# First two units behind each of three norms computed together in two PSUM banks, and the third unit's remainder made before the norm

## What is computed

```
x = x + g1 * rms_norm(y, norm_g[i, 1])                       # y = merged branches @ w_o
h = rms_norm(x, norm_g[i, 2]) * (1 + sc2) + sh2              # norm 1 of the change
x = x + g2 * rms_norm(square(relu(h @ mlp_up)) @ mlp_down, norm_g[i, 3])
...
h = rmsnorm(x, g_mix[l]) * (1.0 + sc1) + sh1                 # norm 2: second block's mixer
x = x + gt1 * hybrid_mixer_2(h, w_in[l], ...)
h = rmsnorm(x, g_ffn[l]) * (1.0 + sc2) + sh2                 # norm 3: second block's FFN
x = x + gt2 * conv_glu_ffn(h, w_ffn_gate[l], w_ffn_up[l], ...)
```

## Time and profile before

| | before |
|---|---|
| median of 3 runs | 3558.66 us (3558.66 to 3563.43) |
| profiled execution | 3559.49 us, its span 3557.8 us |
| mean granted TensorE clock | 0.981 |
| busy: TensorE / VectorE / ScalarE | 3349.8 / 2133.4 / 1159.6 us |
| MLP: first unit starts, third unit starts | 1647.98, 1666.38 |
| MLP: starts of quarters 2, 3, 4 | 1844.99, 2030.67, 2214.61 |
| In2: first unit starts, third unit starts | 2426.27, 2446.86 |
| Ffn2: first unit starts, third unit starts | 2788.17, 2806.15 |
| memsets L2414 and L3052 on VectorE, each | 3.47 us |

### The profile page before, as it was taken

The page is one execution under the profiler, slowest core; times in us unless marked ns, Lnnn a source line. Parts: engine busy times, 40 slices in busy tenths (PEclk is TensorE's granted clock), DMA queues, the critical chain, the costliest instruction groups (busy, mean ns, idle before and its releaser), DMA issues. The chain is left out here.

```text
span 3557.8 us, 57477 instructions
## 1 busy us (share of the span) xinstructions
PE 3349.8 (94%) x23146; PEld 2742.8 (77%) x23146; DVE 2133.4 (60%) x3166; ACT 1159.6 (33%) x1462; POOL 166.9 (5%) x277
## 2 busy tenths in 40 slices
PE   6898989989998999988999999998999899999998
PEld 3673676467777899976888888886888788888887
DVE  2184654653333566556877777777655766666565
ACT  2111031022222322144434343434443444344343
POOL 0000000111221000000000000000000000000000
PEclk9999999999999999999999999999999999999999
DMA  9754624712212587734777777773444455555554
GB/s 370 312 213 164 260 99 172 289 66 82 70 41 82 185 316 308 289 133 155 263 277 272 272 273 279 275 273 103 158 154 155 140 189 189 189 186 185 186 179 138
DMA packets 99122, 706.25 MB, mean 199 GB/s; under 512 B 10992, under 2 KB 10992, under 8 KB 17776
## 3 DMA queue, kind: packets, MB, share of 16 engines
q1 hardware_dynamic: 74736, 523.27, 41.3%
q0 software_dynamic: 23184, 169.88, 13.0%
q10 hardware_dynamic: 1008, 10.23, 0.7%
HBM read 697.05 MB, written 6.29 MB: 198 GB/s over the span
## 5 line engine op out<-in xcount | busy, mean ns | idle before, releaser
L2282 PE MATMUL ps<-hT_parts,rows_parts 128*128 128x512 f32 x3300 | 1170.3, 396 | 0.0
L2281 PE MATMUL ps<-hT_parts,ring_parts 128*128 128x256 f32 x3300 | 934.4, 283 | 3.2 <-DVE hT_parts L2225 3.2
L2247 DVE TENSOR_TENSOR ring_parts<-ring,rows_parts 128x2048 fp32r<-128x2048 f32 (+1 forms) x340 | 769.8, 2265 | 222.4 <-ACT rows_parts L2242 221.5
L2242 ACT ACTIVATE rows_parts<-ring 128x2048 fp32r<-128x2048 f32 (+1 forms) x340 | 643.3, 1894 | 463.6 <-DMA ring<-in_mlp_u 218.3
L2282 PEld LDWEIGHTS ps<-hT_parts,rows_parts 128*128 128x128 f32 x3300 | 624.8, 189 | 128.4
L2281 PEld LDWEIGHTS ps<-hT_parts,ring_parts 128*128 128x128 f32 x3300 | 628.6, 190 | 25.2 <-DVE hT_parts L2225 14.8
L2282 PE MATMUL ps<-work_parts,rows_parts 128*128 128x512 f32 x1616 | 574.5, 397 | 0.0
L2281 PE MATMUL ps<-work_parts,ring_parts 128*128 128x256 f32 x1616 | 453.7, 281 | 0.0
L535 PE MATMUL ps<-hT,ring 128*128 128x512 f32 (+1 forms) x1088 | 377.0, 508 | 16.9 <-ACT work L802 12.6
L2282 PEld LDWEIGHTS ps<-work_parts,rows_parts 128*128 128x128 f32 x1616 | 304.3, 188 | 68.3
L535 PEld LDWEIGHTS ps<-hT,ring 128*128 128x128 f32 x1088 | 207.0, 191 | 185.3 <-issue 173.7
(11 more groups left out here) (432 smaller groups left out, 3627.4 us busy)
## 6 DMA issues: line engine op xcount, KB each, us to landing
ring<-in_mlp_u SPq DMA_DIRECT2D x128, 1024.0 KB, 5.2
ring<-in_ffn_u SPq DMA_DIRECT2D x88, 1024.0 KB, 4.9
rows<-in_mod_r POOLq DMA_DIRECT2D x64, 1024.0 KB, 6.1
ring<-in_gate_u SPq DMA_DIRECT2D x64, 1024.0 KB, 6.6
work<-in_ada_r POOLq DMA_DIRECT2D x64, 1024.0 KB, 5.4
ring<-in_in_u SPq DMA_DIRECT2D x36, 1024.0 KB, 4.9
ring<-in_mod_u SPq DMA_DIRECT2D x32, 1024.0 KB, 7.8
rows<-in_ada_r POOLq DMA_DIRECT2D x32, 1024.0 KB, 7.7
```

Of the source, the lines that this page charges most:

```text
L2242: act.activation(unit_high(u)[:, 0:size], slot(u)[:, 0:size], ACT.Copy).then_inc(hi_done, 1)
L2247: dve.tensor_tensor(ring_parts[:, u % SLOTS, 0:size], slot(u)[:, 0:size], unit_high(u)[:, 0:size].bitcast(F32), ALU.subtract)\
L2281: pe.matmul(ps[:, b, low_half], low, top(kt), start=False, stop=False)
L2282: mm = pe.matmul(ps[:, b, :], high, both(kt), start=False, stop=kt == kts - 1)
```

## The change

`twin_products` does two units K-tile by K-tile, each in its own bank. It waits at its head for both remainders and both banks. It stands for the first two units at three places: in the MLP loop as `n == 0` (thus in each of the four quarters), at the head of In2, and at the head of Ffn2, whose next two units are written out and whose loop begins at 1. The remainder of the third unit is made by VectorE before the norm's reciprocal; inside the MLP loop that of the next quarter's third unit stands at the end of the body.

```
+        def twin_products(pe, u, uses, x, off=0, it=None, k=0, split=0):
+            both, top, low_half = x
+            for o in range(2):
+                pe.wait_ge(w_split, off + (u + o - SPLIT0 + 1))
+                acquire(pe, uses[o], it, k)
+            for kt in range(KT):
+                pe.wait_ge(x_split, split + kt + 1)
+                columns = slice(kt * P, (kt + 1) * P)
+                for o in range(2):
+                    b = uses[o][0]
+                    high, low = w_high[:, (u + o) % SLOTS, columns], ring_parts[:, (u + o) % SLOTS, columns]
...
+                        pe.matmul(ps[:, b, low_half], low, top(kt), start=False, stop=False)
+                        mm = pe.matmul(ps[:, b, :], high, both(kt), start=False, stop=kt == KT - 1)
+                    if kt == KT - 1:
+                        mm.then_inc(w_used, 1)
# Mix.vector
                 add_scaled(dve, own, yT1, gn1)
+                rest_unit(dve, seg_mlp + AHEAD_DVE)
                 rms_x1.vector(dve)
# Mlp.tensor, in the loop over q and n
-                        unit_products(pe, seg_mlp + n, (n % 2, use_mlp[n % 2][1] + n // 2), x, q * (2 * KT), q, KT,
-                                      split=KT if n == 0 else None, ready=hidden_ready)
+                        if n == 0:
+                            twin_products(pe, seg_mlp, use_mlp, x, q * (2 * KT), q, KT, split=KT)
+                        elif n > 1:
+                            unit_products(pe, seg_mlp + n, (n % 2, use_mlp[n % 2][1] + n // 2), x, q * (2 * KT), q, KT, ready=hidden_ready)
# Mlp.vector
-                        if n != KT - 1:
+                        if n not in (0, KT - 1):
                             rest_unit(dve, seg_mlp + n + AHEAD_DVE, q * (2 * KT))
...
+                    rest_unit(dve, seg_mlp + 2 * KT + AHEAD_DVE, q * (2 * KT))
# In2.tensor
-                for n in range(36):
-                    unit_products(pe, seg_in2 + n, in2_use(n), low_then_high(hT_parts), split=2 * KT if n == 0 else None)
+                twin_products(pe, seg_in2, [in2_use(n) for n in range(2)], low_then_high(hT_parts), split=2 * KT)
+                for n in range(1, 36):
+                    if n > 1:
+                        unit_products(pe, seg_in2 + n, in2_use(n), low_then_high(hT_parts))
# Ffn2.tensor
+                    if n == 0:
+                        twin_products(pe, seg_ffn[0], use_ffn[0], low_then_high(hT_parts), split=4 * KT)
+                        for j in range(2, 4):
+                            unit_products(pe, seg_ffn[0] + j, (j % 2, use_ffn[0][j % 2][1] + 1), low_then_high(hT_parts))
-                    with pe.Fori(0, tiles // 2) as it:
+                    with pe.Fori(0 if n else 1, tiles // 2) as it:
# Ffn2.vector
+                rest_unit(dve, seg_ffn[0] + AHEAD_DVE)
                 rms_x3.vector(dve)
```

More of the change, by code:

```diff
@@ L2283, in unit_products @@
             mm.then_inc(w_used, 1)
+        def twin_products(pe, u, uses, x, off=0, it=None, k=0, split=0):
[9 more added lines that the diff above has]
+                    high, low = w_high[:, (u + o) % SLOTS, columns], ring_parts[:, (u + o) % SLOTS, columns]
+                    if kt == 0:
+                        pe.matmul(ps[:, b, :], high, both(kt), start=True, stop=False)
+                        pe.matmul(ps[:, b, low_half], low, top(kt), start=False, stop=False)
+                    else:
+                        pe.matmul(ps[:, b, low_half], low, top(kt), start=False, stop=False)
+                        mm = pe.matmul(ps[:, b, :], high, both(kt), start=False, stop=kt == KT - 1)
+                    if kt == KT - 1:
+                        mm.then_inc(w_used, 1)
         FIRST, SECOND = slice(0, T), slice(T, 2 * T)
@@ L2880, in vector @@
                     t = IN2_ORDER[n]
-                    rest_unit(dve, seg_in2 + n + AHEAD_DVE)
+                    if n:
+                        rest_unit(dve, seg_in2 + n + AHEAD_DVE)
                     large_add(dve, n + 1, n % 2, u2[:, t:t + 1, :], SECOND, in2_half)
@@ L2979, in tensor @@
                 for n, tiles in enumerate(PARTS2):
-                    with pe.Fori(0, tiles // 2) as it:
+                    if n == 0:
[3 more added lines that the diff above has]
+                    with pe.Fori(0 if n else 1, tiles // 2) as it:
                         for j in range(4):
-                            unit_products(pe, seg_ffn[n] + j, (j % 2, use_ffn[n][j % 2][1] + j // 2), low_then_high(hT_parts), it * 4, it, 2,
-                                          split=4 * KT if n + j == 0 else None)
+                            unit_products(pe, seg_ffn[n] + j, (j % 2, use_ffn[n][j % 2][1] + j // 2), low_then_high(hT_parts), it * 4, it, 2)
                     done += tiles
@@ L3074, in hidden @@
                             u = seg_ffn[n] + 2 * r
-                            rest_unit(dve, u + AHEAD_DVE, it * 4, size_of(u + AHEAD_DVE + (2 * tiles - 4 if end else 0)))
+                            if n or r or not begin:
+                                rest_unit(dve, u + AHEAD_DVE, it * 4, size_of(u + AHEAD_DVE + (2 * tiles - 4 if end else 0)))
                             large_add(dve, at + 1, 0, gpad[:, r:r + 1, FFN_TAPS - 1:], SECOND, gate_half)
```

## The result

The changed kernel takes 3574.2 us in the median of 8 runs (3573.13 to 3585.53), the kernel before 3559.41 in the median of 8 (3556.97 to 3570.89). The ratio is 1.0042, 95% interval 1.0030 to 1.0054. The profiled execution took 3573.51 us with a span of 3571.8, where that of before had 3557.8: +14.0 us.

A forecast was written before the change was run, and what follows sets the result against it. VectorE's chain was taken to bound the MLP's up half. Terms +2.2 + 15.7 - 3.4 - 2.2 gave +12.3 on 3559.49 us, 3571.8; with the median 0.8 lower, the forecast was 3571.0 us, range 3565 to 3577.

The forecast's parts named there:

- What bounds the kernel: MLP up half: VectorE's rigid chain needs 11.88 us per pair of units, TensorE 11.2, so VectorE's start sets the quarter's end.
- The three later quarters: MLP loop, quarters two to four: the twin delays the first unit's end and VectorE's chain by 5.24 us each, +15.7 us.
- The first quarter: MLP norm and first quarter: no gain; late row lands later, behind weight transfers, +2.2 us (0 to +4.5).
- a term near +1: First quarter: alternative size if DMA engines alternate between queues and the late row passes the second weight unit.
- In2: Second block's input norm: twin ends both units at 2440.0 instead of 2443.28, -3.4 us.
- FFN: FFN norm: third unit starts 2.2 us sooner, its first bank free only after VectorE's memset, -2.2 us.
- The remainder ahead of the norm: Before the norms' reciprocals: the 2.29 us remainder hides in VectorE's idle time, 2.39 us at the MLP; 0, at most +0.3.
- A sign of being wrong that did come: Changed kernel's trace: a granted clock falling inside the up halves was named as one sign against the forecast.
- A: Whole kernel faster: TensorE's own waits count and VectorE's late start is soaked up; -5.1 us, 3553.6; chance 0.07.
- B: Nearly no change: ScalarE's 1.38 us wait leaves VectorE's chain, so TensorE recovers 4.2 us a quarter; 3558 us; chance 0.07.
- C: Slower, less so: later quarters cost in full, late row on time, In2's clock at once; +8.2 us, 3566.9; chance 0.13.
- D: Worse: late row lands behind both transfers, and transfer pairs collide in each quarter; up to +21, typically 3577 us; chance 0.10.

The follow-up runs named there:

- The stall experiment: Kernel before, with three extra memsets of 2048 elements on VectorE behind the first add of every quarter: 3588.14 us, ratio 1.0073.
- the third version: Kernel before plus In2 and FFN twins, early first late row, two late-row buffers, late columns 5 up, 11 down, none at last two units: 3550.41 us.

## Why the prediction was right, point by point

Forecast 3571.0 (3565 to 3577), measured 3574.2.

- **What bounds the kernel.** Right: VectorE's chain in the up half, 11.88 us a pair against TensorE's 11.2. The stall experiment shows it rigid to 0.1 us.
- **The three later quarters, +15.7.** Right in size and mechanism: 15.74 by the up stretches. From quarter to quarter it shows less cleanly: the third grew by 5.3 us (183.94 to 189.25), the second by 3.8 (185.68 to 189.45), since the kernel before had its stretch at the lower clock there. The first add came 11.56 us after the quarter's start (forecast 11.5). TensorE's wait for the emptied bank after the twin was 0.58 us (0.8), and its waits at odd units began at once, 0.74 at the fourth unit.
- **The first quarter, +2.2.** Right mechanism, mis-sized: 3.24. The late row stood behind two weight units and landed behind both. The rows (SPq is SyncE's queue, POOL issues the late row):

```profile
1662.18 0.92 SPq L275 DMA_DIRECT2D ring<-in_mlp_u  x2
...
1664.68 0.53 POOL L2149 DMA_DIRECT2D work<-in_ada_r  x1 [162.86 <-DVEq L2441]
```
```profile
1673.19 2.29 DVE L2157 CUSTOM_DVE_ANT_0 work<-work,K 128x2048 f32<-128x2048 f32 x1 [6.94 <-DMA work<-in_ada_r]
```

  It took 8.5 us from issue to its reader, where I took 7.5 (between 5.3 and 9.8). The two units landed at 1667.0 and 1670.4 and the row at 1673.2, one behind the other by 3.4 and 2.8 us. The Trainium skill ("DMA: Bandwidth & Descriptors", "Queues, rings and completion order") has each DMA engine take turns between the queues that it has work for, a packet at a time. I had worked out a term near +1 by that, with the row ahead of the second unit; the trace doesn't bear it out, and in the run with the MLP's twin alone the row again came last, 1665.3 to 1674.0. From its start to the next quarter's the first quarter grew by 4.3 us (197.01 to 201.28), still within the 0 to 4.5: 1.0 lies behind the up stretch, most of it in the turn, and the forecast had no term for it.
- **In2, -3.4.** Measured -3.3. The twin took 13.9 us for both units, at a granted clock of 0.50 for the first 5.2 us of it as before. The forecast for them was 13.7.
- **FFN, -2.2.** Measured -2.1: the third unit waits for the first bank's add behind the memset, as forecast.
- **The remainder ahead of the norm, 0.** Right, but barely: the reciprocal's idle time shrank from 2.39 us to 0.19, still ended by ScalarE:

```profile
1642.55 2.29 DVE L2247 TENSOR_TENSOR ring_parts<-ring,rows_parts 128x2048 fp32r<-128x2048 f32 x1
1645.03 1.75 DVE L2203 RECIPROCAL work<-work 128x256 f32<-128x256 f32 x1 [0.19 <-ACT work L2199]
```

- **A sign of being wrong that did come:** I had named a granted clock that falls inside the up halves. In the three later quarters it is 1.00 throughout. In the first it fell to 0.50 twice, at 1664.4 to 1667.8 and at 1674.6 to 1681.5, with TensorE's waits of 2.58 and 6.46 us; before it fell there only in the first unit. VectorE set the pace, and the up stretch grew by the same 3.2 us as the start of the fourth unit, so it cost nothing that can be seen.
- **The rest of the 3.2 us** by which the median lies above the forecast: 1.0 is the late row. In the profiled executions 0.66 came from ahead of the change and +1.4 from outside the stretches of the forecast, less 1.7 at the end; the median of the kernel before was itself 0.75 us higher over eight runs than over three. These are not explained further, and that they nearly cancel is luck.
- **The rivals.** A (TensorE's waits count) and B (ScalarE's wait leaves the chain) are refuted by the 15.74 and by the stall. C needed In2's clock at once and the late row on time; the clock was 0.50 for 5.2 us and the row late. Of D one part was in it, the row's landing; the other, pairs of transfers that collide in each quarter, shows nowhere: the up stretches grew by the 5.2 us and no more.

## What to carry to other kernels

Taking two units together delays the first result by almost a unit. Behind a norm, where TensorE starves anyway, it bought 2 to 3 us at two of the three; at the MLP's norm it bought nothing, since VectorE set the pace behind it. Inside a loop where the data is ready it buys nothing, and the delay is handed on to whoever consumes the first result. Before moving such a result, write down for the consumer "first input + count x pace" against the same for the producer, to the stretch's end: if the consumer comes out last, the delay is paid whole, however idle the consumer looks in the busy shares. And the better change was a smaller one: a fetch asked for some 33 us sooner (3.7 us in the first quarter without the twin, 7.0 with it), with the twins only where the norms are.

## What the runs showed of the hardware

- Three transfers of 1 MB asked for within 2.5 us, on two engines' queues, landed in the order of issue, 4.8, 7.6 and 8.5 us after it. That is no rule: in the kernel before the row of 1764.89 took 7.5 us, and the unit issued 0.16 us behind it 6.7, so it landed first. Alone the late row takes 5.3. At 321 GB/s over a stretch of 93 us (DMA share 0.87) a unit's landing took up to 9.3 us, and 10.2 at the turn of the third version.
- In one version TensorE's clock fell to 0.50 for 3.4 us behind each of three turns in which it had been idle for 2.5 to 3.3 us, and the next unit took 7.1 to 7.2 us instead of 5.6: 1.6 us of the 2.5 gained in each up half went back. Behind turns of 1.4 to 1.6 us it kept 1.00 (88.00 us busy of 88). In another it fell behind turns of 2.04 and 2.36 us and not behind one of 2.23, so what decides in between the runs don't show.
- At the turns of the MLP loop TensorE was idle for 1.35 to 4.10 us (three turns in each of thirteen kernels); at every one a packet of 16 KB on the instruction queue started 2.7 to 3.0 us ahead of its first matmul.
- A memset that waits for the one ahead of it on its own engine starts 0.49 us after that one's end.
- The first 1.65 ms of all but identical code differed by up to 12.9 us between profiled executions of these kernels (MLP start between 1647.84 and 1660.72 us), in the case of the largest some 6 us of it within the first 170 us. The comparison of a stage of its own was sharper than that of whole times.
